# Routed rows of a mixture-of-experts stage: stored in token order and gathered by computed row numbers

## The reference

```
h = modulate(rmsnorm(x), ...)                     # 320 tokens x 1024
g_logits = h @ w_rg + b_rg                        # 4 groups: the best one is taken
e_logits = (h @ w_re + b_re) of that group        # 8 experts: the best two are taken
order = argsort(expert of each of the 640 assignments)
rows = h[token of each assignment], in that order
y = (silu(rows @ w1[e]) * (rows @ w3[e])) @ w2[e] # 32 experts, hidden width 256
out[token] += weight * y                          # two rows for each token
```

## Time and profile before

| | |
|---|---|
| time, median of 3 runs (lowest, highest) | 753.39 us (753.25, 754.41) |
| profiled execution | 751.94 us |
| span of its instructions | 750.2 us |
| PE busy | 613.7 us, 82% |
| PE weight loads busy | 382.8 us, 51% |
| DVE busy | 307.6 us, 41% |
| ACT busy | 190.5 us, 25% |
| POOL busy | 143.8 us, 19% |
| DMA | 233.23 MB, mean 311 GB/s |

### The profile page before, as it was taken

The page is one execution under the profiler, slowest core; times in us unless marked ns, Lnnn a source line. Parts: engine busy times, 40 slices in busy tenths (PEclk is TensorE's granted clock), DMA queues, the critical chain, the costliest instruction groups (busy, mean ns, idle before and its releaser), DMA issues.

```text
span 750.2 us, 11499 instructions
## 1 busy us (share of the span) xinstructions
PE 613.7 (82%) x4484; PEld 382.8 (51%) x4484; DVE 307.6 (41%) x781; ACT 190.5 (25%) x486; POOL 143.8 (19%) x179
## 2 busy tenths in 40 slices
PE   4879998997878999998999970888888778778760
PEld 2456554654565665665668870644444434344320
DVE  1422210213865455774532367244443242333307
ACT  1202000101863445344431160111111111111134
POOL 3030400211011333333200003122222121122140
PEclk9989999999899999999999995899999999999965
DMA  9999866975506699999975098689899999999352
GB/s 311 409 374 304 293 259 265 355 293 181 213 22 250 238 403 403 420 404 420 384 310 227 1 372 340 240 325 402 317 419 417 416 417 416 416 417 415 147 151 71
DMA packets 48607, 233.23 MB, mean 311 GB/s; under 512 B 6452, under 2 KB 6637, under 8 KB 32052
## 3 DMA queue, kind: packets, MB, share of 16 engines
q1 hardware_dynamic: 30242, 145.80, 48.6%
q0 software_dynamic: 15344, 79.96, 28.1%
q10 hardware_dynamic: 2978, 6.88, 2.6%
HBM read 220.51 MB, written 17.87 MB: 318 GB/s over the span
## 4 chain that ended last, share of the span: by engine, by line
PE 47%; DMA 33%; DVE 9%; ACT 3%; issue 2%; POOL 2%; ACTq 1%; SPq 1%; POOLq 0%; DVEq 0%
DMA ring<-w 12%; PE ps L1913 11%; DMA ring<-cache_moba_k,v_row 10%; PE ps L1626 8%; PE ps L1834 5%; PE ps L1738 5%; DMA ring<-w_ada 4%; DMA ring<-w_in 4%; DVE work L1418 2%; PE ps L1523 2%; PE ps L1635 2%; PE ps L1922 2%; PE ps L1990 1%; PE ps L1758 1%; DMA work<-scr_h 1%
## 5 line engine op out<-in xcount | busy, mean ns | idle before, releaser
L1913 PE MATMUL ps<-ring,work 128*64 128x256 f32 x960 | 121.8, 412 | 18.8 <-DMA ring<-w 15.8
L1913 PEld LDWEIGHTS ps<-ring,work 128*64 128x64 f32 x960 | 74.7, 147 | 57.5 <-issue 28.7
L1626 PE MATMUL ps<-xh,ring 128*128 128x320 f32 x256 | 72.2, 440 | 6.5 <-DMA ring<-w_in 6.5
L1418 DVE TENSOR_SCALAR work<-work 128x128 f32<-128x128 f32 x32 | 15.7, 490 | 144.8 <-ACT work L862 144.8
L1738 PE MATMUL ps<-cst,ring 128*128 128x128 f32 x512 | 61.0, 279 | 8.1 <-DMA ring<-cache_moba_k,v_row 3.2
L1738 PEld LDWEIGHTS ps<-cst,ring 128*128 128x128 f32 x512 | 57.3, 143 | 13.4 <-DMA ring<-cache_moba_k,v_row 4.6
L1626 PEld LDWEIGHTS ps<-xh,ring 128*128 128x128 f32 x256 | 48.8, 193 | 28.2 <-DMA ring<-w_in 6.7
L1922 PE MATMUL ps<-ring,work 128*64 128x512 f32 x240 | 56.8, 593 | 0.7 <-ACT work L866 0.7
L1197 DVE COPY work<-ps 128x512 f32<-128x512 f32 x64 | 44.2, 692 | 22.3 <-PE ps L1738 22.3
L609 POOL DMA_INDIRECT scr_y<-work,y_row x32 | 31.4, 981 | 113.4 <-DVE work L1429 104.4
L772 ACT COPY work<-ps 128x512 f32<-128x512 f32 x64 | 37.3, 589 | 35.3 <-PE ps L1738 35.3
(11 more groups left out here) (380 smaller groups left out, 862.8 us busy)
## 6 DMA issues: line engine op xcount, KB each, us to landing
ring<-w SPq DMA_DIRECT2D x90, 1024.0 KB, 12.1
ring<-w_ada SPq DMA_DIRECT2D x4, 4096.0 KB, 13.8
ring<-w_ada SPq DMA_DIRECT2D x4, 2048.0 KB, 13.6
ring<-w_in SPq DMA_DIRECT2D x2, 4096.0 KB, 35.7
ring<-w_in SPq DMA_DIRECT2D x2, 2048.0 KB, 27.8
ring<-w_out SPq DMA_DIRECT2D x1, 4096.0 KB, 18.1
work<-w SPq DMA_DIRECT2D x3, 1024.0 KB, 7.0
scr_y<-work POOLq DMA_DIRECT2D x1, 2304.0 KB, 15.3
```

The lines of the kernel that those rows point to most:

```text
L1418: steps = [lambda: ts(s, s, 1.0, None, ALU.add), lambda: nc.vector.reciprocal(s, s), lambda: tt(s, s, a, ALU.mult), lambda: tt(hid[:, par, ...
L1626: last = mm(ps[r % 4][:, 0:NT], wv[:, k, col:col + P], hT[:, k, :], start=(k == 0), stop=(k == KC - 1))
L1913: last = mm(o, h_cur[:, par, c, :], w[:, c, f], start=(c == 0), stop=(c == KC - 1))
```

## The change

- h_tok is turned and copied before the last two rounds of x (TOK_ROUNDS). GpSimd stores its three tiles with plain DMAs to scr_h, now 320 rows in token order, each when its copies are done.
- The vector engine turns the place of each assignment into a tile number (of 5) and a one-hot of the position within the tile (at_col, 6 x 128 numbers a partition). PE multiplies it with the token numbers (tok_in); the product is, for each sorted position, the number of its token (row_tok). GpSimd gathers five tiles of 128 rows from scr_h with indirect DMAs, each with a semaphore of its own (rows_in), and PE transposes a tile when it has landed.
- The group is chosen with a reduction and compares; experts of other groups get -1e30, and max and max_index go over all 32 expert logits. Fewer and wider matmuls make the ranks (the ones matmul over two tiles at once).
- SP's load of expert 5 waits for the three stores too. The two reads on SP are gone. A constant table (back_no, 64 KB) is loaded by GpSimd at that time.
- The weights wt and the zeroing of h_sort's tail come before the sorted copies, and the overflow tables (from ov_a on) behind them; tabs 1 is signalled before the copies and tabs 2 after the overflow tables. GpSimd starts the experts at tabs 1; SP and GpSimd wait for tabs 2 after all experts.

```diff
@@ -103,6 +104,9 @@
+    tok = P * np.arange(3)[None, :] + k
+    put("tok_no", np.where(tok < NT, tok, 0))
+    put("back_no", (m - P) / P)
@@ -135,7 +139,7 @@
     scr_w = nc.dram_tensor("scr_w", (H, WREP, WROW), F32).ap()
-    scr_h = nc.dram_tensor("scr_h", (ASSIGN, D), F32).ap()
+    scr_h = nc.dram_tensor("scr_h", (NT, D), F32).ap()
     scr_y = nc.dram_tensor("scr_y", (ASSIGN + MAXOV * BLK, D), F32).ap()
@@ -265,31 +269,37 @@
...
+        row_tok = sb("row_tok", [P, ASSIGN // P], U32)
+        NJ = ASSIGN // P
+        at_col = region(16384, 6 * P).rearrange("p (i m) -> p i m", i=6)
+        in_tile = region(17188, 6 * NJ).rearrange("p (i j) -> p i j", i=6)
+        tok_in = region(17218, 6 * NJ).rearrange("p (i j) -> p i j", i=6)
...
@@ -336,10 +346,13 @@
...
+        rows_in = [(k_in[0], 32 * NB), (k_in[1], 32 * NB), (v_in[0], 32 * NB), (v_in[1], 32 * NB), (head_in, 64)]
@@ -378,11 +391,14 @@
+        TOK_ROUNDS = ([(0, t, hf) for t in range(2) for hf in range(2)]
+                      + [(1, t, hf) for t in range(3) for hf in range(2)] + [(0, 2, 0), (0, 2, 1)])
...
-            t, hf = r % 6 // 2, r % 2
+            which, t, hf = TOK_ROUNDS[r]
             n = TILES[t][1]
-            return (x_tok2, h_tok)[r // 6][0:n, t, 512 * hf:512 * hf + 512], ps[4 + r % 4][0:n, :]
+            return (x_tok2, h_tok)[which][0:n, t, 512 * hf:512 * hf + 512], ps[4 + r % 4][0:n, :]
@@ -453,15 +469,12 @@
             sp.wait_ge(S["htok_tp"], 12)
+            sp.wait_ge(S["h_out"], 16 * 3)
             sp.dma_start(w1_of[ES + 1], w1[0, ES + 1].rearrange("(p k) n -> p k n", p=P)).then_inc(exp_in[ES + 1], 16)
...
-            sp.wait_ge(S["h_out"], 16 * 6)
-            hv = scr_h.rearrange("(j p) d -> p j d", p=P)
-            sp.dma_start(h_rows[:, 0:2], hv[:, 0:2]).then_inc(S["h_in0"], 16)
-            sp.dma_start(h_rows[:, 2:], hv[:, 2:]).then_inc(S["h_in1"], 16)
             sp.wait_ge(S["sort_tp"], 2 * (ASSIGN // P))
@@ -483,7 +496,7 @@
                 load_expert(e, k, exp_in[k])
-            sp.wait_ge(S["tabs"], 1)
+            sp.wait_ge(S["tabs"], 2)
             nov = sp.value_load(nov_i[0:1, 0:1], min_val=0, max_val=MAXOV)
@@ -586,15 +599,19 @@
-            pool.wait_ge(S["htok_ev"], 12)
-            for a in range(2):
-                pool.wait_ge(S["slot"], a + 1)
-                for t, (_, n) in enumerate(TILES):
-                    pool.indirect_dma_start(scr_h, bass.IndirectOffsetOnAxis(slotu[0:n, 3 * a + t:3 * a + t + 1], 0),
-                                            h_tok[0:n, t, :], None).then_inc(S["h_out"], 16)
+            pool.wait_ge(S["ssq2"], 2)
+            pool.dma_start(back_no, consts[:, NCONST + NEARLY:]).then_inc(small_in, 16)
+            for t, (t0, n) in enumerate(TILES):
+                pool.wait_ge(S["htok_ev"], 6 + 2 * t)
+                pool.dma_start(scr_h[t0:t0 + n, :], h_tok[0:n, t, :]).then_inc(S["h_out"], 16)
+            pool.wait_ge(S["idx"], 1)
+            pool.wait_ge(S["h_out"], 16 * 3)
+            for j in range(NJ):
+                pool.indirect_dma_start(h_rows[:, j, :], None, scr_h, bass.IndirectOffsetOnAxis(row_tok[:, j:j + 1], 0)
+                                        ).then_inc(rows_in[j][0], 16)
             pool.wait_ge(S["sorted_a"], ASSIGN // P)
             pool.wait_ge(S["sorted_v"], ASSIGN // P)
-            pool.wait_ge(S["tabs"], 2)
+            pool.wait_ge(S["tabs"], 1)
@@ -618,6 +635,7 @@
                 pool.wait_ge(S[f"y_dma{par}"], 16 * NE // 2)
+            pool.wait_ge(S["tabs"], 2)
             nov = pool.value_load(nov_i[0:1, 0:1], min_val=0, max_val=MAXOV)
@@ -1317,51 +1335,54 @@
+            link(nc.vector.memset(lg, 0.0))
+            link(nc.vector.memset(ones32, 1.0))
+            nc.vector.memset(eps_col, EPS)
             v.wait_ge(S["r_mm"], 1)
-            nc.vector.memset(rt[:, 0:72], NEG)
-            link(nc.vector.memset(lg, 0.0))
             for t, (_, n) in enumerate(TILES):
                 link(tt(lg[0:n, t, :], ps[1 + t][0:n, 0:36], brow[0:n, :], ALU.add))
-            link(nc.vector.tensor_copy(g8[:, :, 0:NG], lg[:, :, 0:NG]))
+            link(nc.vector.tensor_reduce(gmax, lg[:, :, 0:NG], AX.X, ALU.max))
+            link(tt(gtop, lg[:, :, 0:NG], gmax.unsqueeze(2).broadcast_to([P, 3, NG]), ALU.is_equal))
+            tt(gex, lg[:, :, 0:NG], gmax.unsqueeze(2).broadcast_to([P, 3, NG]), ALU.subtract
+               ).then_inc(S["lg_ready"], 1)
+            link(stt(gval, gtop, -float(NE), const("iota32")[:, 0:NG].unsqueeze(1).broadcast_to([P, 3, NG]),
+                     ALU.mult, ALU.add))
+            link(nc.vector.tensor_reduce(gmin, gval, AX.X, ALU.min))
+            link(tt(gout, gval, gmin.unsqueeze(2).broadcast_to([P, 3, NG]), ALU.not_equal))
+            link(stt(sel_e.rearrange("p t (g e) -> p t g e", g=NG), gout.unsqueeze(3).broadcast_to([P, 3, NG, EPG]),
+                     NEG, lg[:, :, NG:].rearrange("p t (g e) -> p t g e", g=NG), ALU.mult, ALU.add))
             for t in range(3):
-                link(nc.vector.max(gm8[:, t, :], g8[:, t, :]))
-                link(nc.vector.max_index(gi8[:, t, :], gm8[:, t, :], g8[:, t, :]))
-            link(nc.vector.tensor_copy(gidf, gi8[:]))
-            tt(gex, lg[:, :, 0:NG], gm8[:, :, 0:1].broadcast_to([P, 3, NG]), ALU.subtract).then_inc(S["lg_ready"], 1)
-            link(tt(goh, const("iota32")[:, 0:NG].unsqueeze(1).broadcast_to([P, 3, NG]),
-                    gidf[:, :, 0:1].broadcast_to([P, 3, NG]), ALU.is_equal))
-            for t in range(3):
-                link(tt(sel_e[:, t, :].rearrange("p (g e) -> p g e", g=NG),
-                        lg[:, t, NG:].rearrange("p (g e) -> p g e", g=NG),
-                        goh[:, t, :].unsqueeze(2).broadcast_to([P, NG, EPG]), ALU.mult))
-            link(nc.vector.tensor_reduce(e8, sel_e.rearrange("p t (g e) -> p t e g", g=NG), AX.X, ALU.add))
-            for t in range(3):
-                link(nc.vector.max(em8[:, t, :], e8[:, t, :]))
-                link(nc.vector.max_index(ei8[:, t, :], em8[:, t, :], e8[:, t, :]))
-            link(nc.vector.tensor_copy(eidf, ei8[:]))
+                link(nc.vector.max(em8[:, t, :], sel_e[:, t, :]))
+                link(nc.vector.max_index(ei8[:, t, :], em8[:, t, :], sel_e[:, t, :]))
             tt(tex.unsqueeze(2), em8[:, :, 1:2], em8[:, :, 0:1], ALU.subtract).then_inc(S["lg_ready"], 1)
-            for a in range(2):
-                link(stt(ids[:, a, :].unsqueeze(2), gidf[:, :, 0:1], float(EPG), eidf[:, :, a:a + 1],
-                         ALU.mult, ALU.add))
-                link(tt(A[:, a], const("iota32").unsqueeze(1).broadcast_to([P, 3, NE]),
-                        ids[:, a, :].unsqueeze(2).broadcast_to([P, 3, NE]), ALU.is_equal))
+            link(nc.vector.tensor_copy(ids, ei8[:, :, 0:2].rearrange("p t a -> p a t")))
+            link(tt(A.rearrange("p a t n -> p (a t) n"), const("iota32").unsqueeze(1).broadcast_to([P, 6, NE]),
+                    ids.rearrange("p a t -> p (a t)").unsqueeze(2).broadcast_to([P, 6, NE]), ALU.is_equal))
             link(nc.vector.memset(A[NS:, :, 2, :], 0.0))
...
-            link(nc.vector.memset(ones32, 1.0))
-            nc.vector.memset(eps_col, EPS)
             v.wait_ge(S["rank_mm"], 1)
-            link(nc.vector.tensor_copy(rank, ps[2][:, 0:96].rearrange("p (t n) -> p t n", t=3)))
+            rank_ps = ps[2][:, 0:96].rearrange("p (t n) -> p t n", t=3)
+            link(nc.vector.tensor_tensor_scan(start, ones32, ps[2][:, 96:128], 0.0, ALU.mult, ALU.add))
+            link(tt(start, start, ps[2][:, 96:128], ALU.subtract))
+            link(tt(place_m, rank_ps, start.unsqueeze(1).broadcast_to([P, 3, NE]), ALU.add))
+            link(stt(tmp6.rearrange("p (a t) n -> p a t n", a=2), A, 1.0 / P,
+                     place_m.unsqueeze(1).broadcast_to([P, 2, 3, NE]), ALU.mult, ALU.mult))
+            link(nc.vector.tensor_reduce(frac, tmp6, AX.X, ALU.add))
+            link(tt(past, frac.unsqueeze(2).broadcast_to([P, 6, NJ + 1]),
+                    const("iota32")[:, 0:NJ + 1].unsqueeze(1).broadcast_to([P, 6, NJ + 1]), ALU.is_ge))
+            link(nc.vector.tensor_reduce(whole, past, AX.X, ALU.add))
+            link(tt(in_tile, past[:, :, 0:NJ], past[:, :, 1:NJ + 1], ALU.subtract))
+            link(tt(frac, frac, whole, ALU.subtract))
+            v.wait_ge(small_in, 16 * 7)
+            tt(tok_in.rearrange("p (a t) j -> p a t j", a=2), in_tile.rearrange("p (a t) j -> p a t j", a=2),
+               const("tok_no").unsqueeze(1).unsqueeze(3).broadcast_to([P, 2, 3, NJ]), ALU.mult)
+            tt(at_col, back_no.unsqueeze(1).broadcast_to([P, 6, P]),
+               frac.unsqueeze(2).broadcast_to([P, 6, P]), ALU.is_equal).then_inc(S["slot"], 1)
+            link(nc.vector.tensor_copy(rank, rank_ps))
             link(nc.vector.tensor_copy(cnt, ps[2][:, 96:128]))
-            link(nc.vector.tensor_tensor_scan(start, ones32, cnt, 0.0, ALU.mult, ALU.add))
-            link(tt(start, start, cnt, ALU.subtract))
```

(82 more changed lines are left out.)

4 lines of the change are left out of this document (1 added, 3 removed).

## The result

The changed kernel took 747.08 us, the median of 7 runs (744.85 to 749.17), beside 753.25 us for the kernel before in the same rounds (7 runs, 750.82 to 754.62). The ratio is 0.9924, with a 95% interval of 0.9903 to 0.9945: faster by 5.7 us (4.1 to 7.3). The forecast was 748.8 us, 4.6 us faster. The profiled execution of the changed kernel took 748.04 us, span 746.3.

The account below looks back on a forecast made before the run. A full DMA system was taken to bound the stretch up to the last transpose, which would end 4.6 us earlier: profiled 751.94 to 747.3, plus 1.45 for the median, 748.8 us. Range for 8 in 10: 744.8 to 752.8.

Parts of the forecast that it names:

- Selection, rank, one-hot: Router to index matmuls: selection 2.5 us earlier at 444.8, rank matmuls end at 446.2, one-hot chain takes 3.5 us.
- Index matmuls: TensorE after the one-hot: 12 instructions over 5 columns, 2.0 us taken between 1.3 and 2.5; index stands at 452.0.
- Stores: Three token-order stores of h, 1.31 MB each, under the loads of experts 2 and 3: landed between 449 and 452.7, 452.0 taken.
- Gathers: Five gathers sharing the engines with expert 5: 5.77 MB in 13.8 us, plus 1.4 for slow rows; landed at 469.8.
- X: How much earlier the last transpose ends and expert 0 starts: 4.6 us, least 2.2, most 8.9.
- Tail: Transposes after the last gather lands: one tile left, 1.5 us taken; the last ends at 471.3, against 475.92.
- Tables: Overflow tables moved behind the copies: hidden under expert 0's first matmuls, cost nothing; without that cover up to 4.9 us.
- Clock: TensorE at expert 0's start: about the same 3 us at half clock; 0 taken, bounds 0.6 worse to 1.5 better.
- Train: Experts after 478.44, a fixed train: a start of expert 0 that is X earlier shows at the end as X.
- Rival 1: Gathers get ahead of expert 5's load in the DMA engines: X = 8, 745.4 us; chance 0.22.
- Rivals 2 and 3: Gathers slow beside expert 5: at 150 GB/s X = 1.1, 752.3 us (chance 0.13); at 110 GB/s 758.4 us (chance 0.09).
- Rival 4: GpSimd's gather issue stands still until the vector engine's table chain ends: X = 3.7, 749.7 us; chance 0.06.

Follow-up runs that it names:

- e3: Changed kernel with three more linked compares of 768 elements ahead of the one-hot, index 2.9 us later: 749.37 us (0.9956); run again, 747.5 us (0.9922).
- e2: Changed kernel, but SP's load of expert 5 also waits until all five gathers have landed: 744.67 us, 0.9884 of the kernel before.
- f4: Changed kernel with the overflow tables back ahead of the weights' steps and the sorted copies: 748.11 us, 0.9931 of the kernel before.
- e1: Changed kernel without SP's wait for the three stores ahead of expert 5's load: 746.9 us, 0.9923 of the kernel before.
- e4: Kernel before with only the new router steps and wide rank matmuls, scatter and read back unchanged: 750.87 us (0.9973); run again, 752.44 us (0.9995).

## Why the prediction was right

Its mechanism held: the bytes, not the vector steps, set the last transpose, and the train kept the shift. Step by step, times after T0 (predicted, measured):

| step | predicted | measured |
|---|---|---|
| selection ready | 4.8 | 4.8 |
| rank matmuls end | 6.2 | 6.5 |
| one-hot chain | 3.5 long | 3.5 long |
| index stands | 12.0 | 13.0 |
| stores landed | 12.0 | 13.5 |
| hole in the DMA | 2.5 long | 2.0 long |
| DMA stream ends | 29.0 | 29.0 |
| last transpose ends | 31.3 | 31.9 |
| first refill earlier by | 4.6 | 4.1 |
| end of span earlier by | 4.6 | 5.4 |

- *Selection, rank, one-hot.* Right in size. The forecast had TensorE idle for 1.2 us ahead of the rank matmuls; in fact the turns of h kept it busy until 446.80, and they ended 0.3 later. The one step of 768 elements took 0.95 us, where 1.0 was taken from a row of 512.
- *Index matmuls.* 2.62 us, where 2.0 was taken between 1.3 and 2.5: they ran at the low clock nearly throughout (0.53 over 451.6 to 454.3). No cost of it can be told, as in e3.
- *Stores.* 1.5 us late. The turns of h ran at half clock (last section), so the third store went out at 447.11, 5.6 us after T0. That isn't what made it late: in e2 and f4 the turns ran at the higher level, it went out 4.1 us after T0, and it landed 13.5 and 13.4 us after T0 all the same. The stream of weights and stores ran full until shortly before it landed, and that stream ended 1.6 us later than the sum had it. About 0.8 of this is a stretch with the stores in it, 447.0 to 449.5, which moved 282 GB/s at a share of 0.86, where the sum had 418 throughout.
- *Gathers.* The added 1.4 us for slow rows of 4 KB was wrong: expert 5's 3.15 MB and the gathers' 2.62 passed in 14.3 us, 403 GB/s, 0.5 above their time at 0.418 MB/us. The slowness is there when they are alone (e2: 297 GB/s at a share of 0.92), and hardly shows beside the weights; why wasn't tested. The recorded working has a slip here: at 267 GB/s the 2.62 MB take 9.8 us, not 9, so the upper bound was +3.5 and the least X 1.6. The lower end of its own range, 746.9, is an X of 6.5 and doesn't follow from its bound of 8.9. The 2 us and 436 GB/s of the Trainium skill (DMA: Bandwidth & Descriptors, "Anatomy of one DMA — SWDGE (gpsimd) path") leave this slower part out as well: alone, the trace doesn't agree with that rate; mixed, a sum without a slow term is nearer.
- *Two errors of opposite sign.* Stores and index late by 1.0 to 1.5 and the mixed stream faster by 0.9, with a shorter hole: that the end of the stream came out at 29.0 is partly luck.
- *Tail.* The third of five tiles was still being turned at its end, so three were left and not one: the first two turns began only at 464.38 and 467.12, and a turn took some 1.7 to 2.0 us at half clock. 2.9 us instead of 2.3.
- *Tables.* Hidden: they ran from 474.08 to 479.35, and the sigmoid of expert 0 wanted the vector engine at 481.57. f4 confirms it.
- *Clock.* Taken as no gain and no loss: right, experts 0 and 1 took 8.60 us for their first matmuls, 8.83 before.
- *Train.* The local gain was 4.0 us and the timed one 5.7 (4.1 to 7.3). The difference in the profiles is the train: it takes either 222.5 to 222.8 or 223.8 to 224.1 us in kernels that load expert 3 where it was. The traces show where the 1.3 us lie. In the four long ones (before, e1, the second e3, the second e4) the last expert's 32 first matmuls took 5.36 us, in the seven short ones 3.67. The first row is of before, the second of after:

```profile
703.60 5.36 PE L1913 MATMUL ps<-ring,work 128*64 128x256 f32 x32 [1.29 <-DMA ring<-w]
...
701.63 3.67 PE L1937 MATMUL ps<-ring,work 128*64 128x256 f32 x32
```

  The granted clock was 0.72 over 703 to 709 of before and 1.00 over 701 to 706 of after. Other experts take 5.36 us now and then in every kernel, but the next one then had no wait for weights; behind the last one nothing makes up for it. e3 and e4 each show both lengths in one and the same kernel, so this part isn't the change's doing. What puts the low clock on the last expert wasn't found, and that the timed gain is 1.7 us above the local one isn't explained beyond this.
- *Where the 4.0 us come from.* After T0 the last byte ahead of the last transpose moved at 32.0 us before and at 29.0 now, and the tail behind it went from 3.9 to 2.9 us. Before, 14.68 MB had to pass up to there (12.06 and the read back's 2.62), now 13.37 MB; the 1.31 MB less are 3.1 us at 0.418 MB/us. This is read from the two traces: no run takes these bytes away alone.
- *Rival 1*, the gathers ahead of expert 5, did not occur by itself: in after they landed 10.6 us after their issue, behind it. e2 forces that order and measures it: an end 10.7 us before that of the old kernel in the profiles and 8.7 less in the timing, where the rival had 8.
- *Rivals 2 and 3* fall by the mixed 403 GB/s. *Rival 4*, too: the gathers' issues started every 1.25 to 1.31 us and took 0.94 to 1.00 beside the vector steps, as the scatters did before. Here no run shows the blocking of which the Trainium skill warns (SBUF — State Buffer, "SBUF: two separate sides"). But the vector copy that it names did not stand beside these issues either; products, sums, reductions, a cast and a memset did.
